# Log gates of all sample streams summed at once, new values fetched from the outputs

## The reference

```python
k_all = jnp.concatenate([k_pre, k], axis=1)        # 512 cached keys and 16 new ones, 8 heads of 64
v_all = jnp.concatenate([v_pre, v], axis=1)
lf_all = jnp.concatenate([lf_pre, lf], axis=1)     # log gates, cached and new
c = jnp.cumsum(lf_all, axis=1)
# block():
s = jnp.einsum('bqhd,bkhd->bhqk', q_blk, k_all) * scale
bias = c[queries] - c_k                            # the same for all keys of a head
p = softmax(where(mask, s + bias, -inf));  out = p @ v_all
# window attention of a stream: k_win, v_win = [meta 16 | cached window 128 | new 16], with a learned sink
```

## Time and profile before

| | us |
|---|---|
| runs, median of 3 | 1690.1 (1689.72 to 1690.94) |
| span of the profiled execution, first to last instruction | 1688.2 |
| time of the profiled execution itself | not given beside its span |
| PE busy | 1658.4 (98%) |
| DVE, ACT, POOL busy | 1081.6, 776.5, 318.1 |
| sample streams in the timeline | 578.2 to about 740 |

### The profile page before, as it was taken

The page is one execution under the profiler, slowest core; times in us unless marked ns, Lnnn a source line. Parts: engine busy times, 40 slices in busy tenths (PEclk is TensorE's granted clock), DMA queues, the critical chain, the costliest instruction groups (busy, mean ns, idle before and its releaser), DMA issues.

```text
span 1688.2 us, 27461 instructions
## 1 busy us (share of the span) xinstructions
PE 1658.4 (98%) x9540; PEld 1491.1 (88%) x9540; DVE 1081.6 (64%) x2322; ACT 776.5 (46%) x1632; POOL 318.1 (19%) x486
## 2 busy tenths in 40 slices
PE   8999999999999999999999999999999999999998
PEld 8999999999889989989988999888888888888886
DVE  7556666544899644454445597777877667774744
ACT  6477777865777533342233333222222334443521
POOL 1311111125333211134532220000000000000242
PEclk9999999999999999999999999999999999999999
DMA  5221212221212554464443422444442763444541
GB/s 186 77 61 46 73 47 59 84 92 39 75 52 69 174 164 159 160 209 131 143 144 100 138 80 94 133 139 143 143 133 102 254 220 111 124 156 127 189 162 75
DMA packets 164315, 205.35 MB, mean 122 GB/s; under 512 B 16152, under 2 KB 113240, under 8 KB 164208
## 3 DMA queue, kind: packets, MB, share of 16 engines
q1 hardware_dynamic: 164208, 203.97, 37.8%
HBM read 144.85 MB, written 57.28 MB: 120 GB/s over the span
## 4 chain that ended last, share of the span: by engine, by line
PE 80%; DVE 8%; issue 4%; ACT 4%; POOL 2%; DMA 1%; SPq 0%; ACTq 0%; DVEq 0%; POOLq 0%
PE gb L501 9%; PE gb L2285 5%; PE sc L3168 5%; PE gb L3168 5%; PE gb L2820 4%; PE gb L2656 4%; PE tp L2820 4%; PE sc L2820 4%; PE tp L3168 4%; PE tp L796 3%; PE gb L928 3%; PE gb L929 3%; PE gb L930 3%; PE sc L2444 3%; PE tp L2444 3%
## 5 line engine op out<-in xcount | busy, mean ns | idle before, releaser
L928 PE MATMUL gb<-Xh,wh 128*128 128x384 f32 (+1 forms) x504 | 175.9, 349 | 0.0
L929 PE MATMUL gb<-Xh,wl 128*128 128x384 f32 (+1 forms) x504 | 170.7, 339 | 0.0
L930 PE MATMUL gb<-Xl,wh 128*128 128x384 f32 (+1 forms) x504 | 170.6, 339 | 0.0
L487 POOL TENSOR_TENSOR wl<-raw,wh 128x256 fp32r<-128x256 f32 x168 | 125.4, 778 | 237.0 <-ACT wh L472 176.1
L3292 POOL TENSOR_TENSOR wl<-raw,wh 128x1024 fp32r<-128x1024 f32 x2 | 5.2, 2618 | 564.1 <-ACT wh L3283 564.1
L501 PE MATMUL gb<-Xh,wh 128*128 128x384 f32 (+1 forms) x288 | 104.0, 361 | 0.0
L501 PE MATMUL gb<-Xh,wl 128*128 128x384 f32 (+1 forms) x288 | 97.7, 339 | 0.0
L501 PE MATMUL gb<-Xl,wh 128*128 128x384 f32 (+1 forms) x288 | 97.3, 338 | 0.0
L928 PEld LDWEIGHTS gb<-Xh,wh 128*128 128x128 f32 x504 | 95.1, 189 | 0.1
L929 PEld LDWEIGHTS gb<-Xh,wl 128*128 128x128 f32 x504 | 95.0, 188 | 0.0
L930 PEld LDWEIGHTS gb<-Xl,wh 128*128 128x128 f32 x504 | 94.8, 188 | 0.0
(11 more groups left out here) (546 smaller groups left out, 4773.5 us busy)
## 6 DMA issues: line engine op xcount, KB each, us to landing
zr<-u_scr SPq DMA_DIRECT2D x91, 256.0 KB, 3.0
raw<-in_w_in SPq DMA_DIRECT2D x70, 256.0 KB, 3.3
u_scr<-ustore SPq DMA_DIRECT2D x26, 576.0 KB, 3.6
u_scr<-ustore SPq DMA_DIRECT2D x13, 768.0 KB, 3.2
sig_scr<-sig SPq DMA_DIRECT2D x16, 576.0 KB, 3.1
raw<-in_w_up SPq DMA_DIRECT2D x36, 256.0 KB, 4.9
kc<-in_cache_fox_k SPq DMA_DIRECT2D x8, 1024.0 KB, 5.7
vc<-in_cache_fox_v SPq DMA_DIRECT2D x8, 1024.0 KB, 7.7
```

The lines of the kernel that those rows point to most:

```text
L487: nc.gpsimd.tensor_tensor(wl[U.slot][:, q], raw[U.slot][:, q], wh[U.slot][:, q].bitcast(F32), ALU.subtract).then_inc(w_lo if x == 3 else w ...
L928: nc.tensor.matmul(gb[c][:, 0:x1 - x0], wh[U.slot][:, ws], Xh3[:, k, x0:x1], start=(k == 0), stop=False)
L929: nc.tensor.matmul(gb[c][:, 0:x1 - x0], wl[U.slot][:, ws], Xh3[:, k, x0:x1], start=False, stop=False)
L930: last = nc.tensor.matmul(gb[c][:, 0:x1 - x0], wh[U.slot][:, ws], Xl3[:, k, x0:x1], start=False, stop=(k == KT - 1))
```

## The change

- The log gates of all 8 streams are loaded once into `clf` (four DMAs, near the end of the window stage; 64 columns for each block of 128 tokens), turned by four transposes (`bias_pe`) and summed by DVE in 64 partitions, one for each stream and head, with scans of 256, 256 and 16 (`bias_dve`). The new tokens' gates come into `lf64` by eight DMAs at the end of `pre_sp`.
- Cast and remainder are stored to DRAM (`b_scr`, `bias_sp`), and each stream loads its 8 rows of both into `cs3` (`sam_bias`), issued behind the gate store of the stream before.
- The new values aren't staged and turned: `sam_new` loads them from the outputs `fox_v_s` and `swa_v_s`, a token per partition. So `vTs`, `vbs`, `vst`, `kvn`, `lf16`, `cs`, `one8` go, with GpSimd's copies and the waits on them; the meta rows of `vmn` are written once by DVE.
- A stream has 7 rounds instead of 10: rounds 4, 6 and 7 (nine transposes) go.
- The last stream's `sg_load` waits for the first score chunk instead of the round of log gates.

```diff
             sp.dma_start(O["fox_f_p"][SEQ:KEYS, :], lfT[0:META, 64:72]).then_inc(kb_out, 16)
             sp.dma_start(O["fox_f_s"], lfT[:, 72:80]).then_inc(kb_out, 16)
             load(sp, Unit(U_QB0 + 4), parts_of(U_QB0 + 4))
+            for b in range(STREAMS):
+                sp.dma_start(lf64[HEADS * b:HEADS * b + HEADS, :], lfq[:, S0 + NEW * b:S0 + NEW * b + NEW]).then_inc(logf_in, 16)
...
                         if c == 0 and u_ == 1:
-                            v.wait_ge(vb_kept, 2)
+                            v.wait_ge(tp_full, SWA_PRE + 3)
...
                     sam_caches(sp, Sam(0, 0))
+                    for t in range(4):
+                        sp.dma_start(clf4[:, t, :, :], clg[:, :, t, :].rearrange("b p h -> p b h")).then_inc(logf_in, 16)
...
             sp.wait_ge(sam_free, S.b + 1)
-            sp.dma_start(clf[:, 32 * e:32 * e + 32].rearrange("p (t h) -> p t h", t=4),
-                         clg[bass.ds(S.b, 1), :, :, :].rearrange("o p t h -> p (o t) h")).then_inc(k_in[e], 16)
             for dst, src, s_ in ((kc, cfk, k_in), (vc, cfv, v_in)):
...
+        def sam_new(sp, S):
+            sp.wait_ge(sam_free, S.b + 2)
+            sp.dma_start(vn[0:NEW, :], O["fox_v_s"][bass.ds(S.b * NEW, NEW), :]).then_inc(new_in, 16)
+            sp.dma_start(vmn[48:48 + NEW, :], O["swa_v_s"][bass.ds(S.b * NEW, NEW), :]).then_inc(new_in, 16)
+        def sam_bias(sp, b):
+            for x in range(2):
+                sp.dma_start(cs3[32 * x:32 * x + HEADS, :].bitcast(F32), b_scr[x][bass.ds(b * HEADS, HEADS), :]).then_inc(cs_in, 16)
+        def bias_sp(sp):
+            sp.wait_ge(kv_out, 4 * 96)
+            sp.wait_ge(zero_s, 18)
+            for x in range(2):
+                sp.wait_ge(cum_done, 3 + x)
+                sp.dma_start(b_scr[x], bias[x][:, :].bitcast(F32)).then_inc(cum_out, 16)
+            sp.wait_ge(cum_out, 48)
+            sam_bias(sp, 0)
+        def bias_pe(pe):
+            pe.wait_ge(logf_in, 192)
+            for t in range(4):
+                R = Count(SAM_RB + t // 2)
+                if t % 2 == 0:
+                    pe.wait_ge(tp_free[R.slot], R.half)
+                last = nc.tensor.transpose(tp[R.slot][0:HEADS * STREAMS, P * t:P * t + P], clf[:, 64 * t:64 * t + 64], ident[:, :])
+                if t % 2:
+                    last.then_inc(tp_full, 1)
+        def bias_dve(v):
+            nc.vector.memset(one64[:, :], 1.0).then_inc(cum_done, 1)
+            v.wait_ge(cum_done, 1)
+            for x in range(2):
+                R = Count(SAM_RB + x)
+                v.wait_ge(tp_full, R.n + 1)
+                if x:
+                    v.wait_ge(tp_free[0], SAM_RB // 2 + 1)
+                nc.vector.tensor_tensor_scan(cum[:, 256 * x:256 * x + 256], one64[:, 0:256],
+                                             tp[R.slot][0:HEADS * STREAMS, 256 * x:256 * x + 256],
+                                             cum[:, 255:256] if x else 0.0, ALU.mult, ALU.add).then_inc(tp_free[R.slot], 1)
+            round_read(v, Count(SAM_RB + 1))
+            v.wait_ge(logf_in, 192)
+            nc.vector.tensor_tensor_scan(cum[:, PAST:PK], one64[:, 0:NEW], lf64[:, :], cum[:, PAST - 1:PAST],
+                                         ALU.mult, ALU.add).then_inc(cum_done, 1)
+            v.wait_ge(cum_done, 2)
+            nc.vector.tensor_copy(bias[0][:, :], cum[:, :]).then_inc(cum_done, 1)
+            v.wait_ge(cum_done, 3)
+            nc.vector.tensor_tensor(bias[1][:, :], cum[:, :], bias[0][:, :].bitcast(F32), ALU.subtract).then_inc(cum_done, 1)
+            v.wait_ge(zero_s, 18)
+            nc.vector.tensor_copy(vmn[32:32 + META, :], vball[0:META, 0:P]).then_inc(cum_done, 1)
         def sam_sp(sp, it):
 
             for e in range(2):
...
                 load(sp, ahead(Unit(U_SAM + e, 2, it)), mix_parts(e) if last else cols_gate(10 + e, it, 2))
                 if not (last and e):
                     sam_caches(sp, Sam(it, 1) if e == 0 else Sam(it + 1, 0))
+                sam_new(sp, S)
                 if last and e:
                     for f in range(3):
                         mix_load(sp, f)
                     sp.wait_ge(sig_out, 16 * 15)
-                    sp.wait_ge(tp_full, S.round(4).n + 1)
+                    sp.wait_ge(sc_full, S.chunk(0).n + 1)
                     sg_load(sp, 0, 0)
                     sp.wait_ge(sc_full, S.chunk(1).n + 1)
                     for f in range(3, 8):
                         mix_load(sp, f)
                 gate_store(sp, S.U, S.b + 8)
+                if not (last and e):
+                    done = at(sp, S.chunk(1).n + 1)
+                    apart(sp)
+                    sp.wait_ge(sc_full, done)
+                    sam_bias(sp, S.b + 1)
...
-                vn3 = kvn[:, :].rearrange("p (k n) -> p k n", n=NEW)
-                for dst, src in ((kn3, b_cols(kTs[:, :], 4, S.b)), (vn3, b_cols(vTs[:, :], 4, S.b)),
-                                 (kall[:, META:META + NEW], kbT[:, bass.ds(S.b * NEW + S0, NEW)]),
-                                 (vst[:, 48:64], vbs[:, bass.ds(S.b * NEW, NEW)])):
+                for dst, src in ((kn3, b_cols(kTs[:, :], 4, S.b)),
+                                 (kall[:, META:META + NEW], kbT[:, bass.ds(S.b * NEW + S0, NEW)])):
                     nc.gpsimd.tensor_copy(dst, src).then_inc(s_stage, 1)
                 qz3 = qz[:, :].rearrange("p (j n) -> p j n", j=4)
                 qzs4 = qzs[:, :].rearrange("p (r g q) -> p r g q", r=4, g=2)
...
-            rounds_read(pe, [S.round(j) for j in (0, 1, 2, 3, 5)])
-            pe.wait_ge(s_cs, S.b * 4 + 4)
+            rounds_read(pe, [S.round(j) for j in (0, 1, 2, 3, 4)])
+            pe.wait_ge(s_stage, S.b * 6 + 6)
+            pe.wait_ge(cs_in, S.b * 32 + 32)
...
-            rounds_read(pe, [S.round(j) for j in (6, 7, 8, 9)])
+            rounds_read(pe, [S.round(j) for j in (5, 6)])
             pe.wait_ge(v_in[e], S.it * 32 + 32)
+            pe.wait_ge(new_in, S.b * 32 + 32)
...
-                def turn_f():
-                    R = S.round(4)
-                    pe.wait_ge(tp_free[R.slot], R.half)
-                    for t in range(4):
-                        last = nc.tensor.transpose(tp[R.slot][0:8, P * t:P * t + P], clf[:, 32 * e + 8 * t:32 * e + 8 * t + 8], ident[:, :])
-                    last.then_inc(tp_full, 1)
-
-                def turn_new():
-                    R = S.round(6)
-                    pe.wait_ge(s_stage, S.b * 8 + 8)
-                    pe.wait_ge(tp_free[R.slot], R.half)
-                    for k in range(4):
-                        last = nc.tensor.transpose(tp[R.slot][0:NEW, P * k:P * k + P], kvn[:, NEW * k:NEW * k + NEW], ident[:, :])
-                    last.then_inc(tp_full, 1)
-
-                def turn_vst():
-                    R = S.round(7)
-                    pe.wait_ge(tp_free[R.slot], R.half)
-                    nc.tensor.transpose(tp[R.slot][:, 0:P], vst[:, :], ident[:, :]).then_inc(tp_full, 1)
-                gemm(pe, U, 1, CHUNK_TOK[1], [turn_f, lambda: round_fill(pe, S.round(5), [kw[e][:, :]]),
-                                              turn_new, turn_vst])
+                gemm(pe, U, 1, CHUNK_TOK[1], [lambda: round_fill(pe, S.round(4), [kw[e][:, :]])])
                 sam_scores_pe(pe, S)
                 gemm(pe, U, 2, CHUNK_TOK[2])
...
-            act.wait_ge(zero_s, 20)
-            for j, dst, src in ((5, kall[:, 32:160], slice(0, P)), (6, vn[0:NEW, :], slice(0, NEW))):
-                R = S.round(j)
-                act.wait_ge(tp_full, R.n + 1)
-                nc.scalar.activation(dst, tp[R.slot][src, 0:dst.shape[1]], ACT.Copy).then_inc(tp_free[R.slot], 1)
+            act.wait_ge(zero_s, 18)
+            R = S.round(4)
+            act.wait_ge(tp_full, R.n + 1)
...
-            v.wait_ge(one_set, 1)
-            v.wait_ge(zero_s, 20)
-            R = S.round(4)
-            v.wait_ge(tp_full, R.n + 1)
-            nc.vector.tensor_tensor_scan(cs[:, 0:512], one8[:, :], tp[R.slot][0:8, :], 0.0,
-                                         ALU.mult, ALU.add).then_inc(tp_free[R.slot], 1)
-            round_read(v, R)
-            nc.vector.tensor_copy(lf16[:, :], lfq[:, bass.ds(S.b * NEW + S0, NEW)]).then_inc(s_cs, 1)
-            v.wait_ge(s_cs, S.b * 4 + 1)
-            nc.vector.tensor_tensor_scan(cs[:, 512:528], one8[:, 0:NEW], lf16[:, :], cs[:, 511:512],
-                                         ALU.mult, ALU.add).then_inc(s_cs, 1)
-            v.wait_ge(s_cs, S.b * 4 + 2)
-            nc.vector.tensor_copy(cs3[0:8, :], cs[:, :]).then_inc(s_cs, 1)
-            v.wait_ge(s_cs, S.b * 4 + 3)
-            nc.vector.tensor_tensor(cs3[32:40, :], cs[:, :], cs3[0:8, :].bitcast(F32), ALU.subtract).then_inc(s_cs, 1)
-            R = S.round(7)
-            v.wait_ge(tp_full, R.n + 1)
-            nc.vector.tensor_copy(vmn[32:64, :], tp[R.slot][32:64, 0:P]).then_inc(tp_free[R.slot], 1)
...
-            nc.vector.memset(one8[:, :], 1.0).then_inc(one_set, 1)
```

(56 more changed lines are left out.)

32 lines of the change are left out of this document (12 added, 20 removed).

## The result

The changed kernel takes 1694.3 us (median of 12 runs, 1692.7 to 1697.1), the kernel before 1690.65 us beside it on the same chip (12 runs, 1689.6 to 1692.4). The ratio is 1.0020, 95% interval 1.0013 to 1.0028: slower by 0.2%, 3.7 us. The forecast was 1690.4, +0.3, "no change" within 3.4 us: the range, 1686.0 to 1694.5, held the time by 0.2 us, and the size of the change was missed. The profiled execution took 1693.4 us, its span is 1691.6 (1688.2 before).

What follows compares the result with a forecast made beforehand. The prediction took TensorE, busy for 98% of the span, as the bound, with SP's DMA queue on the path in the window stage. Added to the 1690.1 us median, -6.3 + 3.7 + 1.8 + 1.1 = +0.3 gave 1690.4, range 1686.0 to 1694.5.

Steps and rivals of the forecast that it cites:

- the rival with a late queue: Before stream 1: bias_sp holds SP, so bias and kw land late and stall TensorE; price 2 to 4 us, 1693.9, chance 0.20.
- The eight small DMAs: Before the window stage: log-gate loads in SP's queue delay the first rope move and the chain; +3.7 us, bounds 0 to 5.0.
- after it TensorE is dense again: Window stage: behind the delayed rope chain TensorE has no further waits, so the +3.7 us is not given back.
- The start of stream 0: Summing all streams' log gates at once delays the first stream's K turns and scores; +1.8 us, bounds +0.9 to +3.5.
- I take 0 for both: Stream 0's bias loads and stream 1's kw land just in time, so neither costs TensorE anything; 0 us, little to spare.
- The streams: Streams 1 to 7: nine fewer transposes save 0.90 us each, -6.3 us in all; stream 0 counted separately.
- I let the last transpose hide: Per stream: the last removed transpose, directly before the scores, hides in their start; 0.90 us taken between 0.88 and 1.01.
- the rival of 19.6 us less: All streams: a transpose costs its full 272 ns, so removing nine per stream gives 1678 us; chance 0.03.
- The tail: After the last stream: later gate-tile loads make the prompt's output loads land 2.4 us later; +1.1 us, between 0 and 2.
- the rope delay is absorbed: Window stage: the eight issues find room or TensorE catches up; 1686.7 us, or 1685.6 with the tail hidden; chance 0.19.

Runs made afterwards that it cites:

- experiment 3: Changed kernel, the eight loads ahead of the window stage fed from input x in DRAM, the real ones from SBUF at step 54: 1691.6 us, ratio 1.0010.
- experiment 1: Changed kernel with all eight lf64 loads moved from ahead of the window stage's first move to its step 54: 1688.9 us, ratio 0.9988.
- experiment 2: Changed kernel with four of the eight lf64 loads left in place and four moved to the window stage's step 54: 1691.0 us, ratio 1.0006.
- experiment 4: Changed kernel with the last stream's gate-tile load waiting on the fourth transpose round again, as in the kernel before: 1693.5 us, ratio 1.0017.
- experiment 8: Changed kernel with lf64 loads at step 54, stream 0 handover waits moved and gate tiles early, plus nine transposes put back per stream: 1693.7 us, ratio 1.0018.
- experiment 9: Same as experiment 8, but only the five transposes of the new values put back per stream: 1690.25 us, ratio 0.9998.
- experiment 12: Changed kernel with lf64 loads at step 54, handover waits moved, gate tiles early, and stream 0's K turns one place later: 1685.5 us, ratio 0.9974.

## Why the range held and the size was missed

The time lies at the upper edge of the range, near the 1693.9 of the rival with a late queue, but not for that rival's reason.

- *The eight small DMAs*: the mechanism was right, in every link (no slack, nothing absorbed, GpSimd, ACT, DVE and TensorE in turn). Only "after it TensorE is dense again" was not: it waits three more times, and these waits are why the half clock cost nothing. The size was not: +3.7 forecast, 5.6 measured, outside my upper bound of 5.0. I priced the issue by the row of the same count, 0.46 us from DRAM, while the earlier trace rows had the row of the same kind, the rope move from SBUF to SBUF at 0.62. Even that was low. This is the largest miss, 1.9 us of the 3.1 between forecast and traces.
- *The start of stream 0*: +1.8 forecast, 3.1 measured, in my bounds. The first K turn's wait of 1.94 us was as worked out, and the fourth's 0.79 too (0.6). The step that failed is "I take 0 for both": the scores waited 0.86 for their bias and stream 1 0.39 for kw. The stores went out near the time worked out (591.96 against 586.0 + 5.6), and so did the loads (595.09 against 589.0 + 5.6 = 594.6), but the scores could go only 3.5 us behind the first load's issue, 3.2 behind the second's, where I took the 1.8 of the earlier trace rows. TensorE was there at 597.8, 0.5 later than worked out, 0.2 of it by the fourth turn. In experiment 3, the same code here and with the clock at 1.00, they went 2.5 us behind the first load's issue without a wait, and the start came to 2.1 us; in 1, 2 and 4 (2.7 us each) the half clock held TensorE back. What all five have is the wait for kw, 0.4 to 1.2 us, and from the gate store to the scores of stream 1 they agree within 0.5 us (34.3 to 34.8; before 32.0). So the zero for kw failed in all five, the zero for the bias in one. The 2.0 us fixed per DMA that the forecast takes from the Trainium skill (DMA: Bandwidth & Descriptors, Anatomy of one DMA) are given there for DMAs issued by GpSimd; here SP issues them, and behind the second store, issued at 592.5, it could go on at 595.09, 2.6 us later.
- *The streams*: -6.3 forecast, -7.0 measured. I let the last transpose hide; the pitch of 0.11 holds for it too. The Trainium skill (TensorE: Matmul & The Clock Gate, PE-mode transpose) gives about 275 ns for one of bf16 in a kernel's context. That agrees with the duration of the float32 rows taken out here (272 ns mean), but in a queue with matmuls a transpose costs 0.11 us: experiments 8 and 9 decide against it as a price, and with it against the rival of 19.6 us less.
- *The tail*: +1.1 forecast, +1.3 in the two traces compared, with the landings 1.6 to 2.4 us later as worked out (2.4). That the sums agree so well is luck in part: the late wait accounts for 0.5 of the 1.3, the rest has no place in the change.
- *The rivals*: "the rope delay is absorbed" is refuted by experiments 1 and 2. "The queue before stream 1 is late" was in the right place, with 0.4 us here and up to 1.2 in the same code, under its price of 2 to 4; experiment 12 shows it right behind: 2.3 us.
- *The balance*: with the measured terms my sum gives +5.6 + 3.1 + 0.4 - 7.0 + 1.3 = 3.4 where I had +0.3. The two costs that were too small outweigh the gain that was too small.

## What to carry to other kernels

Price a DMA issue by a row with the same source and target kind, not by one with the same count, and look at what stands right before and right behind the place in its queue: the same issues cost nothing ahead of an instruction that waits and their full time behind it. When two paths are removed together, try each alone: here one covered the other, and the part that looked larger gave next to nothing by itself (0.10 us a stream). Work that is the same for all streams is cheap to sum at once, but it stands at the start, where nothing hides it: the best version (0.26% faster) moved only its small loads and its handovers out of the way.

## What the runs showed of the hardware

- Issue of eight 8 x 16 tiles by SP: 0.35 us each from DRAM, 0.68 from SBUF (0.68 to 0.70 in the ten other traces that have them, at either place). The four loads of all cached log gates (1,024 runs of 32 bytes each) took 7.7 to 8.1 us of SP's queue, off the path here.
- TensorE idle for 1.9 us was followed by half the granted clock for about 3 us in five of ten traces, idle for 2.3 us by some 3 us of it in experiment 12. Around an idle stretch of 5.4 us it was half for 6 us in the kernel after, around one of 5.8 us for about 3 us in experiment 4, the same code there.
- From the first rope move to the last gate store of the window stage it is 155.5 to 156.9 us in all 14 traces, though the move itself stands between 421.8 and 428.3.
